# MLP down projections from seven block products instead of eight, in a two-layer, then hybrid, transformer kernel

## The reference, cut to what matters

```python
def _sqrelu_mlp(h, w1, w2):
    u = jax.nn.relu(h @ w1)        # w1: 1024 x 4096
    return (u * u) @ w2            # w2: 4096 x 1024
...
h = h + _sqrelu_mlp(_rmsnorm(h, mlp_norm_g[i]), mlp_w1[i], mlp_w2[i])
```

## Time and profile before

| | us |
|---|---|
| median of 3 runs | 2152.09 (2152.0 to 2152.99) |
| the profiled execution | 2150.84 |
| its span, first to last instruction | 2149.2 |
| TensorE busy in the span | 2111.7 (98%) |
| mean granted TensorE clock | 0.998 |

### The profile page before, as it was taken

One profiled execution on the slowest core, in us unless ns is written; L12 is line 12 of the kernel. 1 busy time (PEld: TensorE's weight loads), 2 busy tenths in 40 slices (PEclk: granted clock), 3 DMA queues, 4 the chain that ended last, 5 costly groups with the idle time before them and its releaser, 6 DMA issues.

```text
span 2149.2 us, 27349 instructions
## 1 busy us (share of the span) xinstructions
PE 2111.7 (98%) x9798; PEld 1749.3 (81%) x9798; DVE 1237.6 (58%) x1837; ACT 847.6 (39%) x1363; POOL 294.5 (14%) x330
## 2 busy tenths in 40 slices
PE   8999999999999999999999999999999999999998
PEld 6888888788888888777888888877888888888887
DVE  6464554663454553887645445557765456656674
ACT  4433343432222344776322222447662234433342
POOL 3223132300000011443100000302310010000001
PEclk9999999999999999999999999999999999999999
DMA  5232323233333232222233232321223322333332
GB/s 191 74 98 74 98 64 98 70 115 111 117 101 117 89 103 89 89 74 73 93 99 98 88 103 93 104 84 55 74 78 104 90 96 89 112 104 117 98 97 70
DMA packets 58530, 203.53 MB, mean 95 GB/s; under 512 B 6937, under 2 KB 9129, under 8 KB 58448
## 3 DMA queue, kind: packets, MB, share of 16 engines
q1 hardware_dynamic: 54304, 189.82, 28.1%
q0 software_dynamic: 3712, 11.95, 1.7%
q10 hardware_dynamic: 432, 0.66, 0.1%
HBM read 200.27 MB, written 6.06 MB: 96 GB/s over the span
## 4 chain that ended last, share of the span: by engine, by line
PE 90%; DVE 4%; ACT 4%; issue 1%; POOL 0%; DMA 0%; DVEq 0%; ACTq 0%; POOLq 0%
PE bank L520 29%; PE bank L521 28%; PE bank L522 28%; PE bank L755 1%; DVE w_lo L1535 1%; ACT arena L1245 1%; ACT arena_r L1264 1%; ACT w_hi L1055 1%; PE bank L770 1%; PE bank L768 1%; PE bank L734 0%; ACT arena_r L1258 0%; DVE arena L1789 0%; DVE h L1585 0%; POOL arena L2274 0%
## 5 line engine op out<-in xcount | busy, mean ns | idle before, releaser
L1535 DVE TENSOR_TENSOR w_lo<-raw,w_hi 128x1024 fp32r<-128x1024 f32 x354 | 462.4, 1308 | 272.4 <-ACT w_hi L1055 272.1
L520 PE MATMUL bank<-x_hi,w_hi 128*128 128x512 f32 x1552 | 613.7, 395 | 1.4 <-issue 0.7
L522 PE MATMUL bank<-x_hi,w_lo 128*128 128x512 f32 x1552 | 604.5, 390 | 0.0
L521 PE MATMUL bank<-x_lo,w_hi 128*128 128x512 f32 x1552 | 604.1, 389 | 0.0
L1055 ACT ACTIVATE w_hi<-raw 128x1024 fp32r<-128x1024 f32 x354 | 371.2, 1052 | 386.2 <-PE bank L522 385.1
L520 PE MATMUL bank<-arena_r,w_hi 128*128 128x512 f32 (+1 forms) x1040 | 400.1, 385 | 6.0 <-DVE h L1585 2.7
L522 PE MATMUL bank<-arena_r,w_lo 128*128 128x512 f32 (+1 forms) x1040 | 398.0, 383 | 0.0
L521 PE MATMUL bank<-arena_r,w_hi 128*128 128x512 f32 (+1 forms) x1040 | 397.9, 383 | 0.0
L520 PEld LDWEIGHTS bank<-x_hi,w_hi 128*128 128x128 f32 x1552 | 291.5, 188 | 64.2 <-issue 4.2
L521 PEld LDWEIGHTS bank<-x_lo,w_hi 128*128 128x128 f32 x1552 | 291.6, 188 | 61.7 <-issue 3.1
L522 PEld LDWEIGHTS bank<-x_hi,w_lo 128*128 128x128 f32 x1552 | 291.3, 188 | 61.3
(11 more groups left out here) (230 smaller groups left out, 1989.4 us busy)
## 6 DMA issues: line engine op xcount, KB each, us to landing
raw<-in_stream SPq DMA_DIRECT2D x354, 512.0 KB, 3.5
...
bias_strips<-bias_strip_once POOLq DMA_DIRECT2D x12, 320.0 KB, 4.2
...
```

What stands on the lines that cost most here:

```text
L520: pe.matmul(dst, lh, rh, start=start, stop=False, **kw)
L521: pe.matmul(dst, lh, rl, start=False, stop=False, **kw)
L522: return pe.matmul(dst, ll, rh, start=False, stop=stop, **kw)
L1535: dve.tensor_tensor(w_lo[:, s, :], raw[:, s, :], f32(w_hi[:, s, :]), ALU.subtract).then_inc(lo_ready, 1)
```

## The change

Each group's down projection, 1024 x 1024 weights by 1024 x 512 activations, goes by Strassen's scheme in Winograd's form. The activations are taken in 4 pairs of contraction tiles (an even and an odd one, `kk`) and two halves of 256 tokens; the weights of two output tiles (two units, `n`) are four blocks of 128 x 512: even and odd rows by two output tiles. Seven products of 4 x 3 matmuls with 256 columns take the place of eight. They need seven forms of the activations (`B11, T1, B21, B22, T2, T3, T4`, four of which are sums) and seven of the weights (A11, A12, A22 and the sums S1 to S4). The 28 products of a group go to banks 4 to 7, and VectorE takes them into quarters of `h` with 31 additions of 256 columns, counted by `quarter_read`; some products add on to a bank that has already been read once.

GpSimd makes the sums: `combos`, four of 128 x 256 for each pair, and `block_sums`, four of 128 x 512 for each two units. `s1f`, `s2f`, `s4f` have two buffers each; S3 is written over the weights in `raw`. ScalarE and VectorE split each form and each block on its own, half a unit at a time, into 8 slots of half a unit in `w_hi` and `w_lo`. The last three splits of an up phase (j of 5, 6, 7) are replaced by the first six blocks of the down phase, and the first three units of the up phase behind are split at the end of `down_seven`. Going up, VectorE makes max(bank, 0) times `rbc` in one instruction, and ScalarE squares it. The last group's work on finished tiles (`hi_and_square`, `x_lo_of`) moves into `down_seven` as `tile`. The 12 strip copies on GpSimd's queue no longer wait for `lo_ready`; they stand between the groups of `block_sums`. On the host the rows of `w2` are reordered.

The core of the diff (12 leading blanks of each line are cut):

```diff
+B11, T1, B21, B22, T2, T3, T4 = range(7)
...
...
+def combo(kk, b, n=1):
+a = (kk * 7 + b) * QUARTER
+return (arena_r[:, o + a:o + a + n * QUARTER] for o in (0, 14 * S))
+def combo_f(b, n=1):
+if b in (B11, B21, B22):
+    return uf[b != B11][:, 0:n * QUARTER]
+a = (b != T1) * (b - T2 + 1) * QUARTER
+return tf[:, a:a + n * QUARTER]
+def block_at(slot):
+return wh_all[:, slot * BLOCK:(slot + 1) * BLOCK], wl_all[:, slot * BLOCK:(slot + 1) * BLOCK]
+def weights(u, row, k):
+return raw[:, (u + row) % RING, k * BLOCK:(k + 1) * BLOCK]
 pf = [arena[:, n * 1280:(n + 1) * 1280] for n in range(2)]
...
+def product(slot, b, bank, fresh, ready, read=None, combos=None):
+    (wh, wl), (of, count) = block_at(slot), ready
+    wait(pe, of, count)
+    if read is not None:
+        wait(pe, quarter_read, read)
+    for kk in range(4):
+        if combos is not None:
+            wait(pe, combo_lo, combos + 5 * kk)
+        a = kk * P
+        m = mm3(banks[bank][:, 0:QUARTER], (wh[:, a:a + P], wl[:, a:a + P]), tuple(combo(kk, b)),
+                fresh and kk == 0, kk == 3, False)
+    m.then_inc(products_done, 1)
+    at.pe = at.pe + 1
+def down_seven(g):
+    u, made, rd = at.u, g * 20, g * 31
+    product(0, B11, 4, True, (block_lo, made + nth_a11(0)), combos=made + 1)
+    product(2, T1, 6, True, (block_lo, made + nth_s1(0)), combos=made + 2)
+    product(3, B21, 7, True, (block_lo, made + nth_a12(0)), combos=made + 3)
+    product(5, T2, 4, False, (block_lo, made + nth_s2(0)), rd + 1, combos=made + 4)
+    product(6, B22, 6, False, (lo_ready, u + 1), rd + 2)
+    for n in range(1, 4):
+        x, x_old, seen = 4 + n % 2, 5 - n % 2, rd + (7 * n - 2)
+        if n == 1:
+            product(0, B11, x, True, (lo_ready, u + 2))
+            wait(pe, combo_lo, made + 20)
+        else:
+            product(0, B11, x, True, (block_lo, made + nth_a11(n)), seen - 2)
+        product(S3_SLOT[n - 1], T3, x_old, False, (block_lo, made + nth_s3(n - 1)), seen - 1)
+        product(2, T1, 6, True, (block_lo, made + nth_s1(n)), seen)
+        product(3, B21, 7, True, (block_lo, made + nth_a12(n)))
+        product(A22_SLOT[n - 1], T4, x_old, False, (block_lo, made + 6) if n == 1 else (lo_ready, u + 2 * n),
+                seen + 2)
+        product(5, T2, x, False, (block_lo, made + nth_s2(n)))
+        product(6, B22, 6, False, (lo_ready, u + (2 * n + 1)), seen + 3)
+    product(S3_SLOT[3], T3, 4, True, (block_lo, made + nth_s3(3)), rd + 24)
+    product(A22_SLOT[3], T4, 7, True, (lo_ready, u + 8))
+    at.u = at.u + 8
...
     with pe.Fori(0, 3) as i:
-        at.enter(i, 16, 16, 16)
-        proj(us, first=[(u_lo, Lin(base, 8, i))])
-        for _ in range(7):
-            proj(us)
+        at.enter(i, 16, 36, 8)
+        down_seven(Lin(g, 1, i))
         for _ in range(8):
             proj()
...
+def combo_his(kk, b, n, of, count):
+    hi, _ = combo(kk, b, n)
+    wait(act, of, count)
+    act.activation(hi, combo_f(b, n), ACT.Copy).then_inc(combo_hi, 1)
+def block_his(slot, src, freed, of, count, done=block_hi):
+    wait(act, of, count)
+    wait(act, products_done, freed)
+    act.activation(block_at(slot)[0], src, ACT.Copy).then_inc(done, 1)
+def landed(u):
+    return raw_landed[u % RING], (u // RING + 1) * 16
+def mlp_up(g):
+    u, sums, lows = at.u + 8, g * 16, g * 20
     for j in range(KT):
-        split()
+        kk = j // 2
+        if j < 5:
+            split()
+        elif j == 5:
+            block_his(0, weights(u, 0, 0), at.pe, *landed(u))
+            block_his(S3_SLOT[0], weights(u, 1, 0), at.pe, block_sum, sums + 3)
+        elif j == 6:
+            block_his(2, s1f[0], at.pe, block_sum, sums + 1)
+            block_his(3, weights(u, 0, 1), at.pe, *landed(u))
+        else:
+            block_his(5, s2f[0], at.pe, block_sum, sums + 2)
+            block_his(A22_SLOT[0], weights(u, 1, 1), at.pe, *landed(u + 1))
         at.step()
-        wait(act, u_ready, lin(base) + (j + 1))
-        act.activation(uh[j], uf[j % 2], ACT.Copy).then_inc(u_hi, 1)
...
+def down_seven(g, tile=lambda j, read: None):
+    block_his(6, s4f[0], p, block_sum, sums + 4, hi_ready)
+    next_a11(1, p + 1)
+    next_s1(1, p + 2)
+    combo_his(3, T3, 2, combo_sum, sums + 16)
+    next_a12(1, p + 3)
+    next_s2(1, p + 4)
+    for n in range(1, 4):
+        e = p + (7 * n - 2)
+        block_his(6, s4f[n % 2], e, block_sum, sums + (4 * n + 4), hi_ready)
+        tile(2 * n - 2, rd + (7 * n - 2))
+        block_his(S3_SLOT[n], weights(u + 2 * n, 1, 0), p + (0, 10, 21)[n - 1], block_sum, sums + (4 * n + 3))
+        block_his(A22_SLOT[n], weights(u + 2 * n, 1, 1), p + (7, 14, 24)[n - 1], *landed(u + (2 * n + 1)),
+                  hi_ready)
+        if n < 3:
+            next_a11(n + 1, e + 1)
+            next_s1(n + 1, e + 3)
+            next_a12(n + 1, e + 4)
+            tile(2 * n - 1, rd + (7 * n + 3))
+            next_s2(n + 1, e + 6)
+    tile(5, rd + 24)
+    at.u, at.pe = at.u + 8, at.pe + 28
+    split(0, p + 20)
+    tile(6, rd + 28)
+    split(1, p + 23)
+    tile(7, rd + 31)
+    split(2, p + 27)
...
+def last_tile(q, n, gain):
+    return lambda j, read: hi_and_square(q, n, j, gain, quarter_read, read)
+mlp(1, 0, last_tile(2, 2, C_MIX1))
...
+def combo_los(g, kk, b, n, nth):
+    hi, lo = combo(kk, b, n)
+    wait(dve, combo_hi, g * 20 + (5 * kk + nth))
+    dve.tensor_tensor(lo, combo_f(b, n), f32(hi), ALU.subtract).then_inc(combo_lo, 1)
+def block_los(slot, src, of, count, done=block_lo):
+    hi, lo = block_at(slot)
+    wait(dve, of, count)
+    dve.tensor_tensor(lo, src, f32(hi), ALU.subtract).then_inc(done, 1)
+def mlp_up(g):
+    u, made = at.u + 8, g * 20
     for j in range(KT):
-        split()
+        kk = j // 2
+        if j < 5:
+            split()
+        elif j == 5:
+            block_los(0, weights(u, 0, 0), block_hi, made + nth_a11(0))
+            block_los(S3_SLOT[0], weights(u, 1, 0), block_hi, made + nth_s3(0))
+        elif j == 6:
+            block_los(2, s1f[0], block_hi, made + nth_s1(0))
+            block_los(3, weights(u, 0, 1), block_hi, made + nth_a12(0))
+        else:
+            block_los(5, s2f[0], block_hi, made + nth_s2(0))
+            block_los(A22_SLOT[0], weights(u, 1, 1), block_hi, made + 6)
         at.step()
-        scaled(zf[j % 2]).then_inc(tile_read, 1)
-        wait(dve, tile_read, at.t)
-        dve.scalar_tensor_tensor(uf[j % 2], zf[j % 2], 0.0, zf[j % 2], ALU.max, ALU.mult)\
-            .then_inc(u_ready, 1)
-        wait(dve, u_hi, lin(base) + (j + 1))
-        dve.tensor_tensor(ul[j], uf[j % 2], f32(uh[j]), ALU.subtract).then_inc(u_lo, 1)
...
+    def add(bank, j, half, done, behind=None):
+        wait(dve, products_done, p + done)
+        if behind is not None:
+            wait(dve, quarter_read, rd + behind)
+        part = h[:, j, half * QUARTER:(half + 1) * QUARTER]
+        dve.tensor_tensor(part, banks[bank][:, 0:QUARTER], part, ALU.add).then_inc(quarter_read, 1)
...
+    add(6, 1, 1, 2)
+    s1(1)
+    add(7, 0, 0, 3, 1)
+    combo_los(g, 3, T3, 2, 5)
+    a12(1)
+    add(4, 0, 1, 4)
+    s2(1)
+    add(6, 0, 1, 5, 4)
+    for n in range(1, 4):
+        x, x_old, j, k, seen = 4 + n % 2, 5 - n % 2, 2 * n, 7 * n - 2, 7 * n - 2
+        s4(n)
+        add(x, j, 0, k + 1)
+        if n < 3:
+            s3(n)
+        add(x_old, j - 1, 1, k + 2, seen - 4 if n > 1 else 2)
+        if n < 3:
+            a22(n)
+            add(6, j + 1, 1, k + 3)
+            tile(2 * n - 2)
+            a11(n + 1)
+            add(7, j, 0, k + 4, seen + 1)
+            s1(n + 1)
+            add(x_old, j - 1, 0, k + 5)
+            a12(n + 1)
+            add(x, j, 1, k + 6)
+            tile(2 * n - 1)
+            s2(n + 1)
+            add(6, j, 1, k + 7, seen + 6)
+    s3(3)
+    add(6, 7, 1, 22)
+    tile(4)
+    add(7, 6, 0, 23, 20)
+    add(4, 5, 0, 24)
+    a22(3)
+    add(5, 6, 1, 25)
+    add(5, 7, 0, 25)
+    add(5, 7, 1, 25, 22)
+    at.u, at.pe = at.u + 8, at.pe + 28
+    split(0)
+    add(6, 6, 1, 26, 25)
+    tile(5)
+    add(4, 7, 1, 27, 27)
+    add(4, 7, 0, 27, 26)
+    tile(6)
+    split(1)
+    add(7, 7, 0, 28, 30)
+    tile(7)
+    split(2)
...
+def combos(g, kk):
+    made, done = 16 * g + 4 * kk, 20 * g + 5 * kk
+    even, odd = uf
+    t1, t2, t3, t4 = (combo_f(t) for t in (T1, T2, T3, T4))
+    wait(pool, u_ready, 8 * g + 2 * kk + 1)
+    wait(pool, combo_lo, done - 3)
+    pool.tensor_tensor(t1, even[:, QUARTER:S], even[:, 0:QUARTER], ALU.subtract).then_inc(combo_sum, 1)
+    wait(pool, u_ready, 8 * g + 2 * kk + 2)
+    wait(pool, combo_lo, done - 1)
+    wait(pool, combo_sum, made + 1)
+    pool.tensor_tensor(t2, odd[:, QUARTER:S], t1, ALU.subtract).then_inc(combo_sum, 1)
+    wait(pool, combo_lo, done)
+    pool.tensor_tensor(t3, odd[:, QUARTER:S], even[:, QUARTER:S], ALU.subtract).then_inc(combo_sum, 1)
+    wait(pool, combo_sum, made + 2)
+    pool.tensor_tensor(t4, odd[:, 0:QUARTER], t2, ALU.subtract).then_inc(combo_sum, 1)
+def block_sums(g, n, u):
```

(33 more changed lines are left out.)

141 lines of the change are left out of this document (101 added, 40 removed).

## The result

| | before | changed |
|---|---|---|
| median, us | 2152.54 (4 runs, 2152.0 to 2153.17) | 2178.07 (4 runs, 2177.66 to 2179.19) |
| ratio | | 1.0121, 95% interval 1.0105 to 1.0137 |
| span of the profiled execution | 2149.2 | 2176.0 |
| mean granted TensorE clock | 0.998 | 0.995 |

The account below looks back on a forecast made before the run. TensorE's matmul stream was taken to bound the kernel. Three groups at 0.7 us, one at 4.3 and 0.5 behind made 6.9 per MLP, 13.8 for two, giving 2166 us; likeliest 2158 to 2174, range 2131 to 2182.

Parts of the forecast that it names:

- TensorE's part: Each group's down projection: 192 matmuls taking 43.5 us become 336 narrow ones taking 40.3, a gain of 3.2 us.
- The exclusion: VectorE instructions with two SBUF inputs and GpSimd sums exclude each other: 67 of 84 us per group.
- The joint: Up phase to down phase: relu of unit 7 2.7 us late, TensorE stops of 1.5, 0.2 and 1.9 us.
- Inner groups: Three groups per MLP before the last: 3.9 us lost against 3.2 won, each 0.7 us longer.
- Last groups: Each MLP's last group, with 8 `x_lo` (5.3 us) also in VectorE's queue: 4.3 us longer.
- The walk: Hand-tracing the engines' queues through one group in written order, with assumed hand-over times, to find TensorE's stops.
- Behind the MLPs: After each MLP, the next unit waits 0.5 us for the last `x_lo`, where TensorE did not wait before.
- the likeliest case: The forecast itself, whole kernel: 2158 to 2174 us, chance 0.42.
- the third rival: GpSimd becomes the bound at the joints: 14 us longer per MLP, 2180 us, chance 0.18.
- the cover holds: Rival: exclusion falls into idle time or binds less; without it 23 us less, 2129 us, chance 0.28.
- GpSimd as the bound at the joints: Rival: at 1.40 us a sum, three groups lose 2.2 us each, the last 6.7; 2180 us, chance 0.18.
- The signs that I named: Expected profile: TensorE idle 3 to 4 us per phase start, relu 2 to 3 late; wrong if matmuls over 0.125 apart unwaited.

Follow-up runs that it names:

- the fills: Changed kernel with each of GpSimd's sums replaced by three constant fills of the same tile, which read nothing: 2155.04 us, ratio 1.0020 to the kernel before.
- The plain last group: Changed kernel with activation sums on VectorE and each MLP's last group down done as before the change: 2135.88 us, ratio 0.9933 to the kernel before.
- the swap of the last addition: Changed kernel with the last quarter's addition to `h` put ahead of a split on VectorE: 2177.39 us, ratio 1.0124 to the kernel before.
- the kernel with one fill: Changed kernel with each of GpSimd's sums replaced by one constant fill of the same size: 2134.36 us, ratio 0.9921 to the kernel before.

## Why the prediction was right in sign and short in size

**TensorE's part** was right: 40.3 a down phase forecast, 40.4 to 40.6 where nothing stops it. The neighbours' starts of the earlier trace rows were the figure to take.

**The exclusion** was right: 1137 and 1084 ns forecast as above 0.9 us, sums at 1561 to 1738 above 1.29, additions into `h` at 414; and the fills show that it is GpSimd's reading that does it: beside a GpSimd that only writes, the low parts have 686. GpSimd was busy 628 us, not 550, since its sums wait as well.

**The joint** was right to 0.3 us: by the starts, stops of 1.5 to 1.8, 0.2 to 0.3 and 1.9 where 1.5, 0.2 and 1.9 stood. The three inner groups that kept their clock took 44.2 to 44.6, 0.7 to 1.1 more than before, where the forecast had 0.7.

**The failed step is the size of three terms of the sum.**
- *Inner groups*, forecast 6 x 0.7 = 4.2 us, measured 9.7. The missing 5.5 are mostly (4.7) three falls of the granted clock to 0.50. I had priced a stop at its own length and 0.08 for the restart; no row of the kernel before had two stops like these within six microseconds with narrow matmuls behind.
- *Last groups*, forecast 2 x 4.3 = 8.6, measured 5.9 and 7.4, 13.2. The walk had the late additions at 1.6, 0.4, 0.6 and 0.7 us; in the first MLP they were 1.9, 0.5, 1.7 and 0.7. It priced an `x_lo` at its own 0.66 us; six of them in the first MLP's last group had a mean of 0.99, and VectorE was busy 45.6 us of that phase where the walk had 42.1, while beside fills it was 34.9. In the second ScalarE has a third instruction a tile and GpSimd 7 more additions for the second norm, which the walk left out and no run tries by itself: stops of 0.6, 1.4, 0.5, 2.4 and 0.7 us behind the joint.
- *Behind the MLPs*, forecast 0.5 each, measured 0.4 and 4.8. "The unit behind it waits 0.5 for the last `x_lo`" saw the first unit, not the statistics 6 us later that want the last tile's square and GpSimd's sums, nor the half clock behind them. The plain last group took this loss away; the swap of the last addition took 2.3 us of it.

Together 28.1 us for 13.8. So the direction and the mechanism of the joint were right, and the loss was twice the forecast. The band of the likeliest case, 2158 to 2174, misses 2178.07; the wide range holds it because it was drawn around the third rival too, and that is luck.

**The rivals.** That the cover holds fell: it would have been the kernel with one fill. GpSimd as the bound at the joints, 2180, came nearest to the time, but not by its mechanism: it wanted sums of 1.40 us and 2.2 us lost in a group. The 1.48 that spoke for it is GpSimd's mean before:

```profile
L2203 POOL TENSOR_TENSOR acc<-acc,sq 128x512 f32<-128x512 f32 x25 | 37.1, 1482 | 61.1 <-ACT sq L1070 60.4
```

After the change the means are higher still, 1561 to 1738, but the fastest is 1282, so a sum's own time is the 1.29 of the forecast and the rest is waiting; and the stops were those of the forecast. The loss that the rival had for another reason came from the clock and the last groups.

**The signs that I named.** TensorE idle 3 to 4 us at each start held: 3.0 to 3.5 in the inner groups as the profile counts idle time, 3.5 to 4.0 by the starts. Relu of unit 7 came 3.1 us late, inside 2 to 3 but for 0.1. One sign of being wrong did come: the narrow matmuls stood 0.213 apart without a wait, in the stretches at half clock, and that is the term which the sum lacked.
